# A kernel of two transformer blocks with 16 experts: engine orders written anew, a mask added by TensorE

## What is computed

```python
def first_block(x, ...):          # two layers, each x + (o * silu(gate)) @ w_out
    x = stick_breaking_layer(x, l0_norm, l0_w_in, l0_w_out)   # 16 heads of 64, w_in 1024 x 4096: q, k, v, gate
    x = mla_layer(x, l1_norm, l1_w_in, ..., l1_w_out)         # 8 heads of 192, latents of 256 and 128

def second_block(x, c, ctx, ...):
    sh1, sc1, g1, sh2, sc2, g2 = adaln(c, w_mod, b_mod)       # silu(c) @ w_mod, 1024 x 6144
    h = modulate(rmsnorm(x, norm1_g), sh1, sc1)
    q, k, v, hy_in, cf_in = jnp.split(h @ w_in, splits, axis=-1)
    hc = modulate(rmsnorm(ctx, norm1_g), csh1, csc1)          # 256 context tokens
    kc, vc = jnp.split(hc @ w_in[:, D_NA:3 * D_NA], 2, axis=-1)
    attn = neighbourhood_attention(q, k, v, kc, vc, na_rpb)   # 8 heads; table of biases, -1e30 outside the window
    hy = hyena_mixer(hy_in, ...)                              # 3-tap convolution, then two long ones
    cf = conformer_conv(cf_in, ...)                           # GLU, 31-tap convolution, LayerNorm, silu
    x = x + g1 * (jnp.concatenate([attn, hy, cf], axis=-1) @ w_out)
    h2 = modulate(rmsnorm(x, norm2_g), sh2, sc2)
    x = x + g2 * expert_choice_ffn(h2, router_w, w1, w3, w2)  # 16 experts, each its 32 best tokens, ff 2048
    return rmsnorm(x, final_norm_g)
```

## Time and profile before

| | us |
|---|---|
| median of 3 runs (lowest to highest) | 1527.31 (1525.99 to 1527.70) |
| the profiled execution | 1527.65 |
| its span, first to last instruction | 1525.9 |
| PE busy | 1054.2 (69%) |
| DVE (VectorE) busy | 482.1 (32%) |
| ACT (ScalarE) busy | 294.4 (19%) |
| POOL (GpSimd) busy | 81.8 (5%) |
| granted TensorE clock, mean | 0.858 |
| read from HBM | 485.21 MB, 319 GB/s over the span |

### The profile page before, as it was taken

The page is one execution under the profiler, slowest core; times in us unless marked ns, Lnnn a source line. Parts: engine busy times, 40 slices in busy tenths (PEclk is TensorE's granted clock), DMA queues, the critical chain, the costliest instruction groups (busy, mean ns, idle before and its releaser), DMA issues.

```text
span 1525.9 us, 15633 instructions
## 1 busy us (share of the span) xinstructions
PE 1054.2 (69%) x6698; PEld 573.0 (38%) x6698; DVE 482.1 (32%) x889; ACT 294.4 (19%) x493; POOL 81.8 (5%) x86
## 2 busy tenths in 40 slices
PE   6798897979993987865565655666565665656655
PEld 5587685659892775411111111111111111111112
DVE  4845756766468834111010110110110110110103
ACT  5423637544231532000000000000000000000001
POOL 0000700000015200000000000000000000000000
PEclk9899899969996997988888787887987888887878
...
DMA packets 69581, 487.28 MB, mean 319 GB/s; under 512 B 13863, under 2 KB 21576, under 8 KB 42632
## 3 DMA queue, kind: packets, MB, share of 16 engines
...
q10 hardware_dynamic: 1056, 1.05, 0.2%
...
HBM read 485.21 MB, written 1.05 MB: 319 GB/s over the span
## 4 chain that ended last, share of the span: by engine, by line
DMA 54%; PE 29%; DVE 11%; ACT 3%; issue 1%; POOL 1%; DVEq 0%; SPq 0%; ACTq 0%
DMA ring<-in_expert_w 45%; PE ps L266 28%; DMA late<-in_expert_w 8%; DVE ring_r L321 3%; DVE late L1145 2%; ACT ring_r L315 1%; DMA ring<-in_w_in 1%; DVE late L1134 1%; POOL hT L731 1%; DMA ring<-in_l_w_in 0%; DVE hT L455 0%; POOL hT L733 0%; DVE late L443 0%; ACT S L1057 0%; ACT hT L1345 0%
## 5 line engine op out<-in xcount | busy, mean ns | idle before, releaser
L266 PE MATMUL ps<-ring,hT 128*32 128x512 f32 x688 | 118.1, 822 | 87.8 <-DMA ring<-in_expert_w 87.8
L266 PE MATMUL ps<-late_r,ring_r 128*128 128x256 f32 x832 | 161.2, 294 | 20.2 <-DVE hT_r L464 11.7
L266 PE MATMUL ps<-ring,G 128*32 128x512 f32 x672 | 113.6, 811 | 77.5 <-DMA ring<-in_expert_w 77.5
L266 PEld LDWEIGHTS ps<-late_r,ring_r 128*128 128x128 f32 x832 | 137.4, 201 | 24.7 <-DVE ring_r L335 11.6
L321 DVE TENSOR_TENSOR ring_r<-ring,ring_r 128x2048 fp32r<-128x2048 f32 (+1 forms) x44 | 98.9, 2274 | 66.5 <-ACT ring_r L315 66.5
L266 PE MATMUL ps<-hT_r,ring_r 128*128 128x256 f32 x400 | 117.1, 293 | 0.0
L266 PE MATMUL ps<-U_r,ring_r 128*128 128x256 f32 x480 | 108.8, 287 | 0.5 <-DVE hT_r L472 0.4
L266 PE MATMUL ps<-late,U 128*128 128x256 f32 (+2 forms) x402 | 90.5, 532 | 22.9 <-DMA late<-in_expert_w 11.4
L315 ACT ACTIVATE ring_r<-ring 128x2048 fp32r<-128x2048 f32 (+1 forms) x44 | 81.9, 1896 | 80.2 <-PE ps L266 67.8
L266 PE MATMUL ps<-late,G 128*32 128x512 f32 (+1 forms) x384 | 63.8, 741 | 45.1 <-DMA late<-in_expert_w 45.0
L266 PEld LDWEIGHTS ps<-ring,hT 128*32 128x32 f32 x688 | 21.8, 130 | 182.2 <-DMA ring<-in_expert_w 142.7
...
## 6 DMA issues: line engine op xcount, KB each, us to landing
ring<-in_expert_w SPq DMA_DIRECT2D x128, 2048.0 KB, 40.9
...
```

The lines of the kernel that those rows point to most:

```text
L266: mm = lambda e, o, l, r, st, sp_=True, sk=False: e.matmul(o, l, r, start=st, stop=sp_, skip_group_check=sk)
```

## The change

What is computed stays the same, in another order.

- **Layer 0.** Pieces 5 and 6 are the gates now, 7 and 8 the values. The filter steps stand between projections. `pe_sb_z(0)` and `(1)` stand between the four value projections; VectorE and ScalarE score heads 0 to 3 before the loop, for which these heads have their buffers in S and U, and the scores' banks begin at 4.
- **Conversions** move in both lists: chunk 22 and 24 ahead of the second layer's norm, 28 ahead of MLA's modulation step on ScalarE, 29 and 30 to later rounds. `dve_mod(9, ...)` goes into MLA's rounds, `dve_mod(7, ...)` ahead of the residuals; `pe_mod(0)` goes from before `pe_uq` to behind `pe_q_tr`. MLA's scaling of a head is done one round later.
- **Block 2** projects the mixers' inputs first (34 to 36), then values (37 to 40), then the rest. `dve_short` is cut in three and `dve_taps` in three (taps 0 to 11, 12 to 17, 18 to 30), with conversions between.
- **Mask.** It is copied to bf16 once by ScalarE (`maskb`) and added by TensorE, one product more for each unit (16 of 128 x 256). The eight adds of GpSimd are gone.
- **Bias tables.** All eight heads' have their own place (four in the former context buffer CX). Their 32 DMAs are issued in one go, ahead of the two pieces of the output weight.
- **Mixer loop.** 11 rounds. Long convolutions, conformer steps, transposes, scaling and values are each a round later; chunks 42 to 45 are converted in rounds 2 to 5 and not in 5, 6, 8, 9.

Three places of VectorE's list show it. A row is line, operation, output and inputs (`ring` and `ring_r`: weights, the latter as rounded; `ps`: a bank of TensorE's results; `late`, `S`, `U`, `G`, `hT`, `SR`, `PC`, `CX`: SBUF regions; `sm`: statistics); the line numbers of these rows are 1 to 13 higher in the changed file, so L322 is L321 of before, L556 L555, L724 and L728 L715 and L719. First, the end of layer 0's projections, where its attention begins. Before:

The diff, cut to its core:

```diff
     out = [("l0_w_in", 0, 256), ("l0_w_in", 256, 256)]
-    out += [("l0_w_in", a, 512) for a in range(512, 4096, 512)]
+    out += [("l0_w_in", a, 512) for a in (512, 1024, 1536, 3072, 3584, 2048, 2560)]
     out += [("l0_w_out", a, 512) for a in (0, 512)]
     out += [("l1_w_in", 0, 448), ("l1_w_in", 448, 512), ("l1_w_in", 960, 512)]
     out += [("l1_w_out", a, 512) for a in (0, 512)]
-    out += [("w_in_2", 512, 512), ("w_in_2", 1024, 512), ("w_in_2", 2048, 512), ("w_in_2", 2560, 256)]
-    out += [("w_in_2", 1536, 512), ("w_in_2", 0, 512)]
+    out += [("w_in_2", 512, 512), ("w_in_2", 2048, 512), ("w_in_2", 2560, 256)]
+    out += [("w_in_2", 1024, 512), ("w_in_2", 1536, 512), ("w_in_2", 0, 512)]
     out += [("w_out_2", a, 512) for a in (0, 512)]
     return out
...
-    tok(5, "l0_v", 0), tok(6, "l0_v", 2)
-    t(7, "gate_r", 0), t(8, "gate_r", 2)
+    t(5, "gate_r", 0), t(6, "gate_r", 2)
+    tok(7, "l0_v", 0), tok(8, "l0_v", 2)
...
-    sb_e1 = lambda h: R[:, (h % 4) * 384:(h % 4 + 1) * 384]
-    sb_L = lambda h: hT[:, (h % 6) * 384:(h % 6 + 1) * 384] if h % 6 < 5 else R[:, 1536:1920]
+
+    sb_e1 = lambda h: R[:, (h % 4) * 384:(h % 4 + 1) * 384] if h >= 4 else (S, U)[h // 2][:, (h % 2 + 2) * 384:(h % 2 + 3) * 384]
+
+    def sb_L(h):
+        if h < 4:
+            return (S, U)[h // 2][:, (h % 2) * 384:(h % 2 + 1) * 384]
+        return hT[:, (h % 6) * 384:(h % 6 + 1) * 384] if h % 6 < 5 else R[:, 1536:1920]
...
-    def dve_taps(e):
-        e.wait_ge(s["cfg"], 2)
-        n = 0
-        for j in range(31):
+    def dve_taps(e, a, z):
+        if a == 0:
+            e.wait_ge(s["pad"], 4)
+        n = 2 * a
+        for j in range(a, z):
             for c in range(2):
...
                 n += 1
-        for c in range(2):
-            e.wait_ge(s["cf_d"], n - 1)
-            e.tensor_scalar(cy[:, c, :], cy[:, c, :], 0.5, p_("cb", c), ALU.mult, ALU.add).then_inc(s["cf_d"], 1)
-            n += 1
+        if z == 31:
+            for c in range(2):
+                e.wait_ge(s["cf_d"], n - 1)
+                e.tensor_scalar(cy[:, c, :], cy[:, c, :], 0.5, p_("cb", c), ALU.mult, ALU.add).then_inc(s["cf_d"], 1)
+                n += 1
...
     def sp_bias(e, h):
-        if h < 4:
-            e.wait_ge(s["proj"], 36)
-        else:
-            e.wait_ge(s["na_s"], 2 * ((h - 4) // 2) + 2)
+        if h == 0:
+            e.wait_ge(s["proj"], 39)
...
-            e.dma_start(dst, src).then_inc(bias_sem[h % 4], 16)
-
-    def pool_bias(e, h):
-        b3 = na_bias(h).rearrange("p (t k) -> p t k", t=2)
-        e.wait_ge(bias_sem[h % 4], 64 * (h // 4 + 1))
-        if h == 0:
-            e.wait_ge(s["ld_wm"], 16)
-        e.tensor_tensor(b3, b3, wmask.unsqueeze(1).broadcast_to([128, 2, 256]), ALU.add).then_inc(s["bs_add"], 1)
+            e.dma_start(dst, src).then_inc(bias_sem[h // 2], 16)
...
-        e.wait_ge(s["bs_add"], 2 * hp + 2)
+            e.wait_ge(s["bm"], 1)
+        e.wait_ge(bias_sem[hp], 128)
...
         for u, h in us.items():
-            k = mm(e, na_b(u)[:, 0:256], c_("flip"), na_bias(h)[:, t * 256:(t + 1) * 256], False, True, True)
+            mm(e, na_b(u)[:, 0:256], c_("flip"), na_bias(h)[:, t * 256:(t + 1) * 256], False, True, True)
+            k = mm(e, na_b(u)[:, 0:256], identb, maskb, False, True, True)
         k.then_inc(s["na_s"], 1)
...
-            if u == ("W", 22):
-                for h in range(4):
+            if u == ("W", 21):
+                for h in range(8):
                     sp_bias(e, h)
         sp_expert(e, 0)
         sp_expert(e, 1)
-        for h in range(4, 8):
-            sp_bias(e, h)
...
         pe_proj(e, 2, **X0)
+        pe_proj(e, 3, **X0)
+        pe_proj(e, 4, **X0)
+        pe_filters(e, 2)
         pe_rms_sum(e, 1, gc)
-        pe_proj(e, 3, **X0)
+        pe_proj(e, 5, **X0)
+        pe_proj(e, 6, **X0)
         pe_rms_all(e, 1)
-        pe_filters(e, 2)
-        pe_proj(e, 4, **X0)
-        pe_proj(e, 5, **X0)
+        pe_proj(e, 7, **X0)
         pe_filters(e, 4)
+        pe_proj(e, 8, **X0)
         pe_filters(e, 5)
-        pe_proj(e, 6, **X0)
-        pe_proj(e, 7, **X0)
+        pe_proj(e, 9, **X0)
         pe_filters(e, 6)
         pe_filters(e, 7)
-        for g in range(8, 12):
-            pe_tok(e, g, **X0)
-        for g in range(12, 16):
-            pe_proj(e, g, **X0)
-        for step in range(8, 11):
-            pe_filters(e, step)
+        pe_proj(e, 10, **X0)
+        pe_filters(e, 8)
+        pe_proj(e, 11, **X0)
+        pe_filters(e, 9)
+        pe_tok(e, 12, **X0)
+        pe_filters(e, 10)
+        pe_sb_z(e, 0)
+        pe_tok(e, 13, **X0)
+        pe_sb_z(e, 1)
+        pe_tok(e, 14, **X0)
+        pe_tok(e, 15, **X0)
         for i in range(11):
             if 0 <= i - 2 < 8:
                 pe_sb_c(e, 2 * i - 4)
                 pe_sb_c(e, 2 * i - 3)
-            if i < 8:
+            if 2 <= i < 8:
                 pe_sb_z(e, i)
             if 0 <= i - 3 < 8:
                 pe_sb_o(e, i - 3)
...
         pe_lat_tr(e)
-        pe_mod(e, 0)
         pe_uq(e)
         pe_proj(e, 24, **X1)
         pe_proj(e, 25, **X1)
         pe_q_tr(e)
+        pe_mod(e, 0)
+        pe_qr_tr(e)
         pe_mod(e, 1)
-        pe_qr_tr(e)
...
+        for g in range(34, 37):
             pe_proj(e, g, **X2)
-        for i in range(10):
-            if i in (0, 4):
+        pe_tok(e, 37, **XC)
+        pe_tok(e, 38, **XC)
+        pe_tok(e, 39, **X2)
+        pe_tok(e, 40, **X2)
+        for g in range(41, 45):
+            pe_proj(e, g, **X2)
+        for i in range(11):
+            if i in (1, 5):
                 pe_hy_t(e, i // 4)
-            if i == 1:
+            if i == 2:
...
                 pe_na_s(e, i)
+            if 0 <= i - 3 < 8:
+                pe_na_o(e, i - 3)
             if i == 9:
+                e.wait_ge(s["na_e"], 14)
+                pe_proj(e, 45, ready=("sp_lo", lambda c: 16 + c - 3), cs=(4, 5, 6, 7), last=False, **XN)
+            if i == 10:
                 e.wait_ge(s["na_e"], 15)
                 pe_proj(e, 46, ready=("sp_lo", lambda c: 16 + c - 3), cs=(4, 5, 6, 7), last=False, **XN)
+            if i == 1:
+                pe_cf_mean(e)
+            if i == 3:
+                pe_cf_var(e)
             if 0 <= i - 2 < 8:
-                pe_na_o(e, i - 2)
-            if i == 8:
-                e.wait_ge(s["na_e"], 14)
-                pe_proj(e, 45, ready=("sp_lo", lambda c: 16 + c - 3), cs=(4, 5, 6, 7), last=False, **XN)
-            if i == 0:
-                pe_cf_mean(e)
-            if i == 2:
-                pe_cf_var(e)
-            if 0 <= i - 1 < 8:
-                pe_na_t(e, i - 1)
+                pe_na_t(e, i - 2)
...
-        conv(16)
         for j in range(4):
-            dve_gate_r(e, 0, 12 + j, j)
-            dve_mod(e, 6, j)
+            dve_gate_r(e, 0, 8 + j, j)
+            if j == 0:
...
             if j:
                 dve_gate(e, j - 1, j - 1, gt0(j - 1))
+            if j == 2:
+                conv(14)
         dve_gate(e, 3, 3, gt0(3))
+        conv(16)
+        dve_mod(e, 6, 0)
+        dve_mod(e, 6, 1)
+        wait_filters(e)
+        dve_sb_z(e, 0)
+        dve_sb_z(e, 1)
+        dve_mod(e, 6, 2)
+        dve_mod(e, 6, 3)
+        dve_sb_z(e, 2)
+        dve_sb_z(e, 3)
         conv(18)
-        wait_filters(e)
         for i in range(11):
             if 0 <= i - 2 < 8:
...
+        dve_mod(e, 9, 0)
         dve_rk(e)
-        dve_mod0(e)
...
         for i in range(11):
             if i < 8:
                 dve_ml_max(e, i)
-                dve_ml_norm(e, i)
+            if 1 <= i < 9:
+                dve_ml_norm(e, i - 1)
+            if 1 <= i < 4:
+                dve_mod(e, 9, i)
+            if i == 4:
+                dve_mod0(e)
+                dve_gain(e, 0, 1, 0, "norm1")
+                dve_gain(e, 1, 1, 1, "norm1")
             if 0 <= i - 3 < 8:
                 dve_ml_o(e, i - 3)
-            if i in (5, 7):
-                conv(29 + (i > 5))
...
         for i in range(4):
             dve_mod(e, 11, i)
+        dve_gain(e, 2, 4, 0, "norm2")
         conv(37)
-        dve_gain(e, 2, 4, 0, "norm2")
+        dve_glu(e)
+        dve_short(e, 0)
+        dve_taps(e, 0, 12)
         conv(39)
-        dve_glu(e)
+        dve_taps(e, 12, 18)
         conv(41)
-        dve_short(e)
-        dve_taps(e)
-        for i in range(10):
-            if i == 1:
+        dve_short(e, 1)
+        dve_short(e, 2)
+        dve_taps(e, 18, 31)
+        for i in range(11):
+            if i == 2:
                 dve_hy_mul(e, 0)
-            if i == 3:
+            if i == 4:
                 dve_hy_gate(e, 0)
-            if i == 5:
+            if i == 6:
                 dve_hy_mul(e, 1)
-            if i == 6:
...
-        for h in range(4):
-            pool_bias(e, h)
         pool_hy_mul(e, 0)
-        for h in range(4, 6):
-            pool_bias(e, h)
         pool_hy_mul(e, 1)
-        for h in range(6, 8):
-            pool_bias(e, h)
```

221 lines of the change are left out of this document (113 added, 108 removed).

## The result

The changed kernel takes 1460.26 us (median of four runs, 1459.71 to 1464.94) against 1527.46 of the kernel before (median of four runs; 1527.31 is that of the first three); the ratio is 0.9569 with a 95% interval of 0.9548 to 0.959. The forecast was 1459, within 1443 to 1482. The profiled execution took 1459.78 us, 67.9 less than the one of before.

The account below looks back on a forecast made before the run. TensorE's path was taken to bound the kernel before 602 us, and the expert-weight DMA stream after it. Stage terms summed to −72.3 us, −68.3 after 4 us taken back for clock, giving 1459 us, range 1443 to 1482.

Parts of the forecast that it names:

- Layer 0: Up to the first cumulative product: five larger stalls and two half-clock stretches go, −29.4 us, bounds −16.3 and −30.4.
- MLA's loop: 297.6 to 344.4 us: idle shrinks by 6 us and clock gives 9.6, together −15.7, bounds 0 and −24.
- mixer loop: Block 2's loop: mask products 3.5 us, more idle in an eleventh round, some clock back; net +3.3, bounds −5 and +9.
- allowance for clock: 4 us taken back from the gain, because remaining waits may still be followed by half clock.
- The join: Expert loads behind the first nine stream at full bandwidth; their start moves with TensorE, so time saved before reaches the end.
- Layer 1's two plus terms: pe_mod(0) moved, so the wait at L831 grows, +1.9 us; two conversions ahead of key transposes' evictions at MLA's entry, +3.7.
- The time of 1455 us: Whole kernel by the clock-gate rule alone: TensorE denser everywhere, so the 4 us of clock are not lost.
- SyncE: 32 bias transfers take 36 us to issue; first output weight issued at about 407 us, some 9 to spare, priced at nothing.
- B: Rival: stalls in MLA and the mixers re-form, MLA's −15.7 becomes 0 and the mixers +3 more; 1478 us, chance 0.22.
- C: Rival: the MLA and mixer loops lose their waits as well, about 15 us idle and 4 of clock; 1440 us, chance 0.10.
- D: Rival: expert loads do not follow TensorE, so the change does not reach the end; 1527 us, chance 0.02.
- E: Rival: output weights stand behind 32 small transfers in SyncE's queue; slower, 1540 us at 3.9 us an issue, chance 0.03.

Follow-up runs that it names:

- clock_fill: The changed kernel with 61 more TensorE products that nothing reads, in its four waits around the router; 1458.09 us.
- b2_only: The kernel before with only the block 2 part of the change (projections, taps, mask, bias rows, eleven mixer rounds); 1510.58 us.
- loop10: The changed kernel with the ten-round mixer loop of before, conversions 42 to 45 in rounds 5, 6, 8, 9; 1455.06 us.
- mask_pool: The changed kernel with the mask added by GpSimd's eight adds again and TensorE's 16 mask products gone; 1467.39 us.
- loop10_fill: loop10 with the 61 unread TensorE products of clock_fill added; 1453.97 us.

## Why the prediction was right

By its steps, in the trace of the changed kernel (a stage's gain is the difference of the same event's start in both):

| step | forecast | measured |
|---|---|---|
| layer 0 to the first cumulative product (156.03 to 126.65) | −29.4 | −29.4 |
| attention loop | −2.4 | −2.4 |
| layer 1's projections | −11.2 | −11.8 |
| pe_mod(0) and the wait at L831 | +1.9 | +3.4 |
| MLA's entry | +3.7 | +4.9 |
| MLA's loop | −15.7 | −16.1 |
| projections and taps (481.7 to 409.8 for the last tap) | −20.8 | −20.5 |
| mixer loop | +3.3 | +7.3 |
| half clock behind it | −1.7 | −1.6 |
| router to first expert product | 0 | +0.7 |
| allowance for clock | +4.0 | in the rows above |
| the stream, and the end behind it | 0 | +0.2 − 2.6 |
| sum (span) | −68.3 | −67.9 |

- **The join** held: the stream behind the ninth load took 902.6 us, so all of the lead reached the end.
- **Layer 0** was the safest term, because it replaced waits by products of a known length: five stalls and two half clocks.
- **Layer 1's two plus terms** were 2.7 us short. The half clock at 208.6 and 256.4, of 4.36 and 4.92 us busy, costs 4.6 by half of its busy time, so it more than covers them: the 4 us of allowance had their place here. The time of 1455 us, which I had worked out from the Trainium skill's page "TensorE: Matmul & The Clock Gate", section "Part 1: The HAM clock gate", with no clock lost, did not come: TensorE is denser in the stage, and its clock still fell in the wait of 5.3 us, behind one of 1.6 and, in MLA's loop, behind two of 0.9 and 1.3. The rule itself, clock by recent busyness, agrees with clock_fill, where 61 products in the waits raised the clock from 0.53 to 0.82. How much clock a wait costs no row here foretells: b2_only has 0.92 where the same loop has 0.98.
- **MLA's loop** came out right by two errors that cancel. I had 6 us less idle and 9.6 of clock. Its 46.8 us before and 30.7 now (first row below, and the third of the stages above) have 14.4 and 5.5 us idle, 8.9 less, and 7.2 less busy time: the idle shrank more, and half clock is left at the loop's end, from 290.5 us on.
- **The mixer loop** is the mis-sized term: +7.3 for +3.3, inside its bounds. By the terms as written it should read +4.0 (3.5 + 16.5 − 13.3 − 2.7); +3.3 comes out with the 14.0 us idle of the loop's whole 71.7 us. Measured, TensorE is busy 58.0 us before (second row) and 58.2 now, so the products and the clock cancel, and idle for 13.7 and 20.7: the whole miss is idle, 7.0 us more where I had 2.5 to 3.2. loop10 shows where it comes from: the new loop order costs 5.2.

```profile
297.60:344.40 46.80, 32.43 (x139) 23.30 (x137) 31.39 (x90) 22.53 (x54) 0.00 (x0) 0.71 0.25 97
...
481.70:553.35 71.65, 57.96 (x401) 45.86 (x401) 50.93 (x108) 34.70 (x66) 11.64 (x9) 0.93 0.18 23
```

- **The mask products**, taken at 3.5 us, were 4.4 busy, 0.27 each:

```profile
L267 PE MATMUL ps<-b 128*128 128x256 bf16 x16 | 4.4, 273 | 0.0
```

- **The adds of GpSimd at nothing** was wrong in its reason. That no wait of TensorE ends on them does not make them free: in the kernel before, operations at L1134 beside them took 1.92 and 2.09 us and not 1.0, just ahead of the taps for which TensorE waited. Put back beside the 16 products they lengthen the wait behind the taps by 2.6 us, and the whole by 4.6 with intervals that overlap; with the products gone as well it is 7.1.
- **SyncE**: the first output weight was issued at 402.54 us (forecast 407), landed at 416.4 and was first read at 426.8: 10 us to spare, 9 forecast. The 32 issues took 29.7 us, 0.93 each.
- **The end** is luck. Behind the last landing there are 21.7 us before and 19.1 after, with the same instructions:

```profile
1504.23:1525.90 21.67, 11.24 (x50) 6.19 (x50) 9.62 (x19) 6.87 (x12) 0.00 (x0) 0.69 0.14 48
```

```profile
1438.90:1458.00 19.10, 8.62 (x50) 4.30 (x50) 9.61 (x19) 6.87 (x12) 0.00 (x0) 0.82 0.15 55
```

A half-clock stretch of 6.8 us stands some 20 us before the end in three profiles (before, mask_pool, loop10_fill) and not in the other eleven. The loop's shortfall and this gain partly cancel, so the 1 us between forecast and median is better than the steps were.

Of the rivals, B (the loops' stalls re-form) was right about the mixer loop, 4.0 us above the forecast where B had 3, and wrong about MLA's; C (the loops lose their waits as well) was wrong about the mixer loop, with 20.7 us idle; D is out, as the issue moved with TensorE; E needed 3.5 us an issue (by 370 us and the 416 at which the cover ends, that is 66 us late and not over 68), and it took 0.93.
